# Six gate halves made at the boundaries behind an FFN instead of inside its chunks

## The reference

```python
mod = (cs @ ada_w[l] + ada_b[l]).reshape(bn, N_SUB, 3, D_MODEL)
shift, scale, gate = mod[:, :, 0, None], mod[:, :, 1, None], mod[:, :, 2, None]
u = x * (1.0 + scale[:, 0]) + shift[:, 0]
y = _swiglu(u, ffn_w13[l, 0], ffn_w2[l, 0])
x = _layer_norm(ALPHA * x + 0.5 * gate[:, 0] * y, ln_g[l, 0], ln_b[l, 0])
# then the mixer (attention, sparse attention, mLSTM, S5) with row 1 of mod,
# and a second FFN with row 2
```

## Time and profile before

| | us |
|---|---|
| median of 3 runs | 1102.37 |
| lowest, highest run | 1101.9, 1108.33 |
| profiled execution, its own time | 1108.7 |
| its span, first to last instruction | 1106.4 |
| mean granted clock of TensorE | 0.98 |

### The profile page before, as it was taken

How to read it: one execution, slowest core, us unless ns; L and a number is a source line. 1 busy time by engine, 2 the same in 40 slices (tenths; PEclk the granted TensorE clock), 3 DMA queues, 4 the chain that set the end, 5 groups by cost and what they waited for, 6 DMA issues and landing times.

```text
span 1106.4 us, 17046 instructions
## 1 busy us (share of the span) xinstructions
PE 1055.8 (95%) x6885; PEld 926.5 (84%) x6885; DVE 908.1 (82%) x1523; ACT 423.1 (38%) x574; POOL 34.9 (3%) x56
## 2 busy tenths in 40 slices
PE   1999999999999999999999999999999999999995
PEld 1899989987865799999989989998787569999994
DVE  6798999978888898988878999888797689755555
ACT  0445334323452433334343543341246244333331
POOL 1000000003000000000000000000300000000000
PEclk9999999989989999999989999999999999999998
DMA  9899998952364688897866895987125257464540
GB/s 368 284 311 326 311 306 298 299 145 77 115 209 140 209 303 305 310 324 277 303 229 212 301 308 184 317 315 197 49 99 186 80 185 260 165 227 149 196 152 39
DMA packets 184585, 250.84 MB, mean 227 GB/s; under 512 B 25452, under 2 KB 133296, under 8 KB 183484
## 3 DMA queue, kind: packets, MB, share of 16 engines
q1 hardware_dynamic: 184508, 249.76, 66.2%
HBM read 248.69 MB, written 1.05 MB: 226 GB/s over the span
## 4 chain that ended last, share of the span: by engine, by line
PE 80%; DVE 11%; DMA 3%; ACT 3%; issue 2%; SPq 1%; POOL 0%; POOLq 0%; DVEq 0%; ACTq 0%
PE PS L616 12%; PE PS L617 12%; PE PS L615 12%; PE PS L734 8%; PE PS L639 6%; PE PS L643 6%; PE PS L642 6%; PE PS L960 2%; PE PS L741 2%; DMA xn<-in_ada_w_dram 2%; PE PS L550 2%; DVE w_in_lo L1131 2%; PE PS L577 2%; PE PS L578 1%; PE PS L586 1%
## 5 line engine op out<-in xcount | busy, mean ns | idle before, releaser
L617 PE MATMUL PS<-u_hi,w_in_lo 128*128 128x256 f32 x1280 | 359.9, 281 | 0.0
L616 PE MATMUL PS<-u_lo,w_in_hi 128*128 128x256 f32 x1280 | 359.1, 281 | 0.0
L615 PE MATMUL PS<-u_hi,w_in_hi 128*128 128x256 f32 x1280 | 358.8, 280 | 0.0
L615 PEld LDWEIGHTS PS<-u_hi,w_in_hi 128*128 128x128 f32 x1280 | 241.7, 189 | 1.8
L616 PEld LDWEIGHTS PS<-u_lo,w_in_hi 128*128 128x128 f32 x1280 | 240.5, 188 | 1.6
L617 PEld LDWEIGHTS PS<-u_hi,w_in_lo 128*128 128x128 f32 x1280 | 240.2, 188 | 0.0
L1131 DVE TENSOR_TENSOR w_in_lo<-w_in_ring,w_in_hi 128x2048 fp32r<-128x2048 f32 x88 | 201.3, 2290 | 28.9 <-ACT w_in_hi L1775 28.9
L1775 ACT ACTIVATE w_in_hi<-w_in_ring 128x2048 fp32r<-128x2048 f32 x88 | 168.0, 1914 | 3.7 <-DMA w_in_ring<-in_ffn_w_dram 3.7
L1768 ACT ACTIVATE arena<-PS 128x256 f32<-128x256 f32 x88 | 33.8, 385 | 293.1 <-PE PS L617 270.0
L639 PE MATMUL PS<-w_out_hi,h_parts 128*128 128x512 f32 x320 | 131.8, 412 | 2.9 <-DVE h_parts L1125 2.9
L1786 ACT ACTIVATE w_out_hi<-w_out_ring 128x1024 fp32r<-128x1024 f32 x80 | 80.6, 1055 | 130.5 <-PE PS L643 130.5
(11 more groups left out here) (314 smaller groups left out, 1283.7 us busy)
## 6 DMA issues: line engine op xcount, KB each, us to landing
w_in_ring<-in_ffn_w_dram SPq DMA_DIRECT2D x88, 1024.0 KB, 7.7
arena<-in_ada_w_dram SPq DMA_DIRECT2D x30, 2048.0 KB, 8.3
w_out_ring<-in_ffn_w_dram SPq DMA_DIRECT2D x44, 1024.0 KB, 6.4
w_in_ring<-in_w_in_dram SPq DMA_DIRECT2D x6, 1024.0 KB, 6.7
w_in_ring<-in_w_in_dram SPq DMA_DIRECT2D x10, 512.0 KB, 5.2
w_out_ring<-in_w_out_dram SPq DMA_DIRECT2D x4, 1024.0 KB, 8.4
w_in_ring<-in_w_in_dram SPq DMA_DIRECT2D x2, 2048.0 KB, 8.7
w_in_ring<-in_w_out_dram SPq DMA_DIRECT2D x4, 1024.0 KB, 6.0
```

The source lines that it names most:

```text
L615: pe.matmul(y, hi, u_hi[:, kt, :], start=(i == 0), stop=False)
L616: pe.matmul(y, hi, u_lo[:, kt, :], start=False, stop=False)
L617: mm = pe.matmul(y, lo[:, kt, half, :], u_hi[:, kt, :], start=False, stop=(i == KT - 1))
```

## The change

Six gate halves (blocks 6, 7, 18, 19, 24, 25) are no longer spread inside chunks. They get accumulators of their own, which lie in the `gate_bc` halves that they later fill; TensorE spreads them at the boundary behind the FFN beside which they were added up, into PSUM banks 4 and 5, and ScalarE copies them there. At each of the three boundaries the third and fourth sums with the second spread between them now stand between the two halves of the transposes, as the sums of the second FFN's boundary did before. One unread product goes at each boundary behind a first FFN, two at the one behind the second FFN of layer 0. On ScalarE the first copy stands ahead of the copy of `cT` (or ahead of `normalise`), the second between the two halves of `normalise`.

```diff
--- before.py
+++ after.py
@@ -82,11 +82,12 @@
 ADA = {(0, 0): dict(zip(range(10), range(0, 10))), (0, 1): dict(zip(range(10), range(12, 22))),
        (1, 0): dict(zip((0, 1, 2, 3, 4, 7, 8, 9), range(22, 30))), (1, 1): dict(zip((0, 1), (30, 31)))}
 
-SUM_ORDER = (0, 1, 6, 7, 8, 9, 2, 3, 4, 5, 10, 11, 12, 13, 18, 19, 20, 21, 14, 15, 16, 17, 24, 25, 22, 23, 26, 27, 28, 29, 30, 31)
+SUM_ORDER = (0, 1, 8, 9, 2, 6, 3, 4, 7, 5, 10, 11, 12, 13, 20, 21, 14, 18, 15, 16, 19, 17, 22, 24, 23, 26, 25, 27, 28, 29, 30, 31)
 SUMMED = {n: i + 1 for i, n in enumerate(SUM_ORDER)}
-IN_CHUNK = (0, 1, 6, 7, 8, 9, 12, 13, 18, 19, 20, 21, 24, 25, 30, 31)
-
-ACC_AT = dict(zip((2, 3, 4, 5, 14, 15, 16, 17, 22, 23, 26, 27, 10, 29), (2, 3, 4, 5, 2, 3, 4, 5, 2, 3, 4, 5, 1, 1)))
+IN_CHUNK = (0, 1, 8, 9, 12, 13, 20, 21, 30, 31)
+
+ACC_AT = dict(zip((2, 3, 4, 5, 14, 15, 16, 17, 22, 23, 26, 27, 10, 29, 6, 7, 18, 19, 24, 25),
+                  (2, 3, 4, 5, 2, 3, 4, 5, 2, 3, 4, 5, 1, 1, 6, 7, 6, 7, 8, 9)))
 TURN_ORDER = [0, 1, 4, 5, 2, 3, 6, 7]
 U_ORDER = [0, 4, 1, 5, 2, 6, 3, 7]
 KEEP_BUSY = True
@@ -220,7 +221,8 @@
         hs, hn = (work_flat[:, 1536 + 512 * k:2048 + 512 * k].rearrange("p (t h e) -> p t h e", t=2, h=H) for k in range(2))
         sc = sb("sc", [P, 384])
 
-        accs = [acc, acc_2, sig_o[:, :, :].rearrange("p a n -> p (a n)"), qk_tanh[:, 0:AW], qk_tanh[:, AW:2 * AW], arena[:, 4096:4608]]
+        accs = [acc, acc_2, sig_o[:, :, :].rearrange("p a n -> p (a n)"), qk_tanh[:, 0:AW], qk_tanh[:, AW:2 * AW], arena[:, 4096:4608],
+                gate_bc[1][:, 0:AW], gate_bc[1][:, AW:2 * AW], gate_bc[0][:, 0:AW], gate_bc[0][:, AW:2 * AW]]
         m8 = sb("m8", [P, 2, 8])
         small = sb("small", [P, 32, 8])
         PS = ctx.enter_context(nc.psum_tensor("PS", [P, 8, 512], F32))
@@ -558,6 +560,11 @@
                     pe.wait_ge(sem("prm_ready"), 1 if n < ADA[1, 0][0] else 2)
                 pe.matmul(PS[:, 7, :], ones[:, :], acc[:, :], start=True, stop=True).then_inc(sem("ada_summed"), 1)
 
+            def spread_late(n, bank):
+
+                pe.wait_ge(sem("acc_step"), n * 8 + 8)
+                pe.matmul(PS[:, bank, :], ones[:, :], acc_of(n), start=True, stop=True).then_inc(sem("ada_summed"), 1)
+
             def first_in(l, f):
 
                 slot = ff_group(f, 0) % 2
@@ -687,7 +694,7 @@
                 release_out(0)
 
                 pe.wait_ge(sem("b_blk_ready"), l * 4 + 4)
-                pe.wait_ge(sem("gate_ready"), (4, 10)[l])
+                pe.wait_ge(sem("gate_ready"), (2, 8)[l])
                 for k in range(2):
                     for t in range(2):
                         mm = pe.transpose(PS[:, 7, (2 * k + t) * P:(2 * k + t + 1) * P],
@@ -697,18 +704,25 @@
                     pe.wait_ge(sem("mod_ready"), 1)
                 pe.wait_ge(sem("h_done"), l * 44 + 24)
                 early = ((2, 3, 4, 5), (22, 23, 26, 27))[l]
-                for i in range(2):
-                    ada_sum(early[i], PS[:, 6, 4 * i:4 * i + 4])
-                keep_busy(1)
+                gates = ((6, 7), (24, 25))[l]
+                ada_sum(early[0], PS[:, 6, 0:4])
+                spread_late(gates[0], 4)
+                ada_sum(early[1], PS[:, 6, 4:8])
                 pe.wait_ge(sem("c_blk_ready"), l * 2 + 2)
                 pe.wait_ge(sem("bbT_ready"), l + 1)
                 for k in range(2):
                     for t in range(2):
                         mm = pe.transpose(PS[:, 7, (2 * k + t) * P:(2 * k + t + 1) * P], c_blk[:, k, t, :], ident[:, :])
                 mm.then_inc(sem("c_turned"), 1)
-                for i in range(2, 4):
-                    ada_sum(early[i], PS[:, 6, 4 * i:4 * i + 4])
-                turn(xn, l, 0)
+
+                def others():
+
+                    ada_sum(early[2], PS[:, 6, 8:12])
+                    spread_late(gates[1], 5)
+                    ada_sum(early[3], PS[:, 6, 12:16])
+
+                turn(xn, l, 0, 0, others)
+                pe.wait_ge(sem("gate_ready"), (4, 10)[l])
                 pe.wait_ge(sem("mod_ready"), (2, 7)[l])
                 pe.wait_ge(sem("cT_ready"), l + 1)
 
@@ -974,19 +988,20 @@
                 if l + 1 < DEPTH:
                     release_out(1)
                     pe.wait_ge(sem("h_done"), l * 44 + 46)
+                    pe.wait_ge(sem("gate_ready"), 6)
+                    pe.wait_ge(sem("mod_ready"), 4)
+                    ada_sum(14, PS[:, 6, 0:4])
+                    spread_late(18, 4)
+                    ada_sum(15, PS[:, 6, 4:8])
+
+                    def others():
+
+                        ada_sum(16, PS[:, 6, 8:12])
+                        spread_late(19, 5)
+                        ada_sum(17, PS[:, 6, 12:16])
+
+                    turn(xn, l, 2, 0, others)
                     pe.wait_ge(sem("gate_ready"), 8)
-                    pe.wait_ge(sem("mod_ready"), 4)
-                    for i, n in enumerate((14, 15)):
-                        ada_sum(n, PS[:, 6, 4 * i:4 * i + 4])
-                    keep_busy(1)
-
-                    def other_sums():
-
-                        for i, n in enumerate((16, 17)):
-                            ada_sum(n, PS[:, 6, 4 * i + 8:4 * i + 12])
-
-                    turn(xn, l, 2, 0, other_sums)
-                    keep_busy(1)
 
 
         @block.vector
@@ -1747,19 +1762,21 @@
                         a.wait_ge(sem("uT_act"), turned // 2 + (j + 1))
                         a.activation(u_hi[:, j, :], uT_lo[:, j, :], ACT.Copy).then_inc(sem("uT_high_act"), 1)
 
-            def normalise(l, s):
+            def normalise(l, s, between=None):
 
                 n = l * 3 + s
                 for tt, cols in ((0, slice(0, D)), (1, slice(512, D))):
+                    if tt == 1 and between is not None:
+                        between()
                     a.wait_ge(sem("nmr_ready"), n * 2 + (tt + 1))
                     a.activation(xn[:, tt, cols], xn[:, tt, cols], ACT.Identity, bias=nmr[:, tt:tt + 1],
                                  scale=rstd[:, tt:tt + 1]).then_inc(sem("xn_act"), 1)
 
-            def copy_gate(n):
+            def copy_gate(n, bank=7):
 
                 s, hf = divmod(gate_of(n), 2)
                 a.wait_ge(sem("ada_summed"), SUMMED[n])
-                a.activation(gate_bc[s % 2][:, hf * 512:(hf + 1) * 512], PS[:, 7, :], ACT.Copy, scale=1.0 if s % 3 == 1 else 0.5
+                a.activation(gate_bc[s % 2][:, hf * 512:(hf + 1) * 512], PS[:, bank, :], ACT.Copy, scale=1.0 if s % 3 == 1 else 0.5
                              ).then_inc(sem("gate_ready"), 1)
 
             def silu_tile(ft, tile):
@@ -1797,10 +1814,10 @@
                             a.wait_ge(sem(f"w_in_loaded{1 - slot}"), in_loads(l, ff_group(f, c + 1)))
                         w_in_high(1 - slot, ft, tile + (2 + ft))
                 if not last:
-                    if c - 1 in ADA[l, f] and gate_of(ADA[l, f][c - 1]) is not None:
+                    if c - 1 in ADA[l, f] and ADA[l, f][c - 1] in IN_CHUNK and gate_of(ADA[l, f][c - 1]) is not None:
                         copy_gate(ADA[l, f][c - 1])
                     w_out_high(l, f, c + 1)
-                elif c - 1 in ADA[l, f] and gate_of(ADA[l, f][c - 1]) is not None:
+                elif c - 1 in ADA[l, f] and ADA[l, f][c - 1] in IN_CHUNK and gate_of(ADA[l, f][c - 1]) is not None:
                     copy_gate(ADA[l, f][c - 1])
 
             def first_weights():
@@ -1826,9 +1843,10 @@
 
                 a.wait_ge(sem("bb_turned"), l + 1)
                 a.activation(bbT[:, :, :, :].rearrange("p a b c -> p (a b c)"), PS[:, 7, :], ACT.Copy).then_inc(sem("bbT_ready"), 1)
+                copy_gate((6, 24)[l], 4)
                 a.wait_ge(sem("c_turned"), l + 1)
                 a.activation(cT[:, :, :, :].rearrange("p a b c -> p (a b c)"), PS[:, 7, :], ACT.Copy).then_inc(sem("cT_ready"), 1)
-                normalise(l, 0)
+                normalise(l, 0, lambda: copy_gate((7, 25)[l], 5))
                 evac_uT(1, l * 24 + 8, l * 3 + 2)
 
 
@@ -1977,7 +1995,9 @@
                     a.wait_ge(sem("w_in_loaded0"), in_loads(l + 1, 0))
                     for ft in range(2):
                         w_in_high(0, ft, ff_tile(l + 1, 0, 0) + ft)
-                normalise(l, 2)
+                if l + 1 < DEPTH:
+                    copy_gate(18, 4)
+                normalise(l, 2, (lambda: copy_gate(19, 5)) if l + 1 < DEPTH else None)
                 if l + 1 < DEPTH:
                     evac_uT(0, l * 24 + 24, l * 3 + 4, l * 2 + 2)
```

## The result

The changed kernel takes **1113.02 us** (median of 10 runs, 1106.13 to 1115.15) against 1102.42 (10 runs, 1101.66 to 1108.59): a ratio of 1.0074, 95% interval 1.0056 to 1.0091. A second set of 5 runs on another occasion gave 1108.75 against 1103.71, ratio 1.0062 (1.0037 to 1.0086). It is slower, by less than 1%. Two executions far outside the others, 3671.8 us of the kernel before and 1685.61 of its variant with one more unread product, are left out of the ratios.

What follows compares the result with a forecast made beforehand. TensorE, busy 95% of the span, was taken as the bound. -3.4 + 3.7 + 3.0 + 3.3 = +6.6 us gave 1115.3 from the profile, 1109.0 from the median; 1112 was chosen between them, range 1101 to 1118.

Steps and rivals of the forecast that it cites:

- The chunk term: In the FFN chunks: removing six spread products from TensorE gives back 3.4 us of span, bounds 2.2 and 5.2.
- The hole: At each boundary: TensorE idles 1 to 2 us ahead of the first transposes, waiting for ScalarE's normalise.
- The boundary terms: Boundaries behind layer 0's first FFN, its second, and layer 1's first get longer: +3.7, +3.0, +3.3 us.
- Two of my signs: At boundaries: clock low as long as before or longer; last transposes 2 to 4 us later, from last output product.
- Rival 1: At the boundaries: TensorE's clock stays high, so the change gains 5.4 us, 1103 from the profile; chance 0.14.
- The rule weighed: At boundaries: two moved 512-column products are more activity than one unread of 384, so the clock could stay up.
- Rival 2: At the boundaries: TensorE has room, so only the chunks' 3.4 us show, 1099 from the median; chance 0.08.
- rival 3: Clock returns so late at all three boundaries that first mixer and input products run slow: 1117, up to 1119; chance 0.20.

## Why the prediction was right

The forecast was 1112 us, slower by less than 1%; measured were 1113.0 and 1108.8. The chunk term, the place and the length of the holes came out. The clock did not: by the prediction's own sign ("I am wrong if the clock stays high through a boundary") it was wrong there, since the clock stayed high through the first boundary in both profiles, and that the total lies so near 1112 is partly luck.

**The chunk term** (-3.4): measured -3.5 in the trace, by its parts 1.46, 1.71 and 0.36 against 1.2, 1.7 and 0.5, and about -3.1 without the 0.40 that lies ahead of the change. Weighing VectorE's busy time against the chunk was what took it from 5.2 to this.

**The hole** was named with its place and length: 1.9 us forecast and 1.90 measured at the first and third boundary, 1.1 and 1.12 at the middle one. The 0.6 us of copy between the halves of normalise shows where the clock was high, as said, and is hidden at the third boundary, where it was low.

**The boundary terms** (+3.7, +3.0, +3.3) vary with the clock from trace to trace. From first piece to first product behind, the three took 10.2, 9.9 and 11.0 before and 11.0, 12.2 and 13.4 in the second profile of the changed kernel: +0.8, +2.3, +2.4. The first of them is the term that I sized wrong: I took the low clock for granted there, and it was high in both profiles. Measured against the profile of before the three make 5.5 us, not 10.0, and that profile is of one of the longest executions (1108.7). Two of my signs failed with it: the low stretches were no longer than before (none, 6.8 and 6.8 us in the first profile, none, 10.2 and 10.2 in the second, against 6.8, 10.2 and 10.2), and the last transposes ended 0.6, 0.7 and 1.6 us later in the first profile, where I had said 2 to 4. The sum came out all the same because I had placed it between the one worked from the profile (1115.3) and the one from the median (1109.0), for no reason that a row showed. With the chunks' 3.1 to 3.5 the runs put the boundaries' loss at 8 to 14 us; the forecast was 10.0. The runs of before had a mean granted clock of 0.983 against 0.980 in the profile that I worked from, which fits a larger loss in the runs than between the profiles; that it is the reason wasn't tested.

**Rival 1** (the clock holds) came half true: it held at the first boundary, and even so that boundary wasn't shorter (11.0 against 10.2), since I had counted neither the 0.6 us hole in that sum nor the product's full 0.94; these make 0.7 of the 1.1 us by which I was off. **The rule weighed**, that activity releases the throttle ("TensorE: Matmul & The Clock Gate", Part 1, of the Trainium skill): the runs agree in direction. Unread products in the holes gave 5 to 9 us back, with a mean granted clock of 0.990 against 0.980. What I had right is that the hole speaks against the change. The moved products were not enough to hold the clock at all boundaries, as the rival had it, and the holes' own length and the work behind them remained. **Rival 2** (free products) and **rival 3** (1117 and more) didn't happen; 1115.15 was the slowest run.

What stays open: why the same kernel's runs differ by 9 us. The clock's low stretches differ from execution to execution (their place and their length), and mean clock and time go together in the ten runs (0.989 at 1106.1, 0.974 at 1115.2), but no run here sets where they fall. Open too is how the loss at the boundaries divides between the order and the added products: each experiment changes the clock as well.

## What to carry to other kernels

An operation moved from a busy stretch into a boundary is only free if nothing stands between it and the work that releases the boundary: look at what the copying engine has to do next, and which work now fills the wait of the engine that is the bound. Here taking two sums and a product out from behind a wait, at two boundaries, gave 7 to 11 us, while cutting all six products to one column gave 0 to 4. With that order and the copies behind both halves of normalise the changed kernel is 0.3 to 0.4% faster than the kernel before. Where a stretch of TensorE is thin, compare many runs, not two profiles: runs of one kernel lay 9 us apart here, as much as the change did. And compare at the same mean clock: a cure that raises the clock (here unread products) doesn't show that the clock was the cause.

## What the runs showed of the hardware

Work that nobody reads can pay: unread products in the changed kernel's holes made it 5 to 9 us faster, with no dependence changed. Low stretches of the clock of 3.4, 6.8, 10.2 and 13.7 us were seen in these profiles; those at the boundaries began behind stretches of sums of single columns and holes, and ended behind transposes or products that followed each other closely. That TensorE is shown as busy did not hold the clock: in the kernel before it fell at 236.7, behind two sums and an unread product, in a window of 1 us in which TensorE was busy throughout.
